# A PEER layer on one NeuronCore: u in hi and lo parts from the first gate group on, one-hot rows made by eight small VectorE operations

## What is computed

```python
q = (t @ q_w).reshape(n, PEER_H, 2, PEER_DQ // 2)
s = einsum('thpd,hpnd->thpn', q, sub_keys)
...                                   # top 16 of the 128 keys on each side, top 16 of their sums
gates = softmax(top_s)
act = gelu(einsum('chkd,cd->chk', u_tab[i_c], x_c))
out = einsum('chk,chkd->cd', g_c * act, v_tab[i_c])
```

## Time and profile before

| | |
|---|---|
| median of 3 runs | 2286.87 us (2285.64 to 2291.26) |
| span of the profiled execution | 2288.8 us |
| busy in it | TensorE 92%, its weight loads 80%, VectorE 60%, ScalarE 42%, GpSimd 10% |
| u loop, first picks to last block | about 1396 to 1910 us |
| of it with gate groups | about 1592 to 1872 us |
| v loop | about 1910 to 2270 us |

### The profile page before, as it was taken

How to read it: one execution, slowest core, us unless ns; L and a number is a source line. 1 busy time by engine, 2 the same in 40 slices (tenths; PEclk the granted TensorE clock), 3 DMA queues, 4 the chain that set the end, 5 groups by cost and what they waited for, 6 DMA issues and landing times.

```text
span 2288.8 us, 34365 instructions
## 1 busy us (share of the span) xinstructions
PE 2108.4 (92%) x12479; PEld 1839.2 (80%) x12479; DVE 1375.4 (60%) x2074; ACT 959.0 (42%) x1885; POOL 234.4 (10%) x219
## 2 busy tenths in 40 slices
PE   6999899977899999879999879999999999999996
PEld 6876788877798879868888778777999988777775
DVE  5535677677766662154544555998555566666665
ACT  4443433458543443133333332112554454555554
POOL 2101000001000000200000000000345551000000
PEclk9999999998999999969999989999999999999998
DMA  7542566644547853300000453444434345666664
GB/s 251 184 183 91 198 236 222 221 148 148 202 159 259 278 184 106 92 29 1 1 1 8 123 109 98 135 137 148 127 122 120 120 120 185 192 187 190 191 187 135
DMA packets 212839, 333.49 MB, mean 146 GB/s; under 512 B 23654, under 2 KB 141148, under 8 KB 212584
## 3 DMA queue, kind: packets, MB, share of 16 engines
q1 hardware_dynamic: 209320, 321.20, 44.2%
q0 software_dynamic: 3392, 10.52, 1.3%
HBM read 330.58 MB, written 1.08 MB: 145 GB/s over the span
## 4 chain that ended last, share of the span: by engine, by line
PE 68%; DVE 16%; PEld 7%; ACT 3%; issue 3%; DMA 1%; SPq 1%; PEldq 1%; DVEq 0%; ACTq 0%
PE psum L2204 14%; PE psum L2205 14%; PE psum L2206 14%; PE psum L2725 10%; PEld psum L2204 2%; PEld psum L2205 2%; PE psum L2766 2%; PEld psum L2206 2%; DVE weights_lo L1546 2%; PE psum L2616 2%; PE psum L2622 2%; DVE u_turned L2145 1%; DVE u_turned_more L2145 1%; PE psum L2597 1%; DVE top_at L2079 1%
## 5 line engine op out<-in xcount | busy, mean ns | idle before, releaser
L1546 DVE TENSOR_TENSOR weights_lo<-weights,weights_hi 128x1024 fp32r<-128x1024 f32 (+2 forms) x336 | 345.3, 1085 | 261.9 <-ACT weights_hi L1078 257.0
L2204 PE MATMUL psum<-input_hi,weights_hi 128*128 128x256 f32 x1288 | 371.6, 289 | 19.1 <-DVE weights_lo L1546 6.1
L2205 PE MATMUL psum<-input_lo,weights_hi 128*128 128x256 f32 x1288 | 367.8, 286 | 0.0
L2206 PE MATMUL psum<-input_hi,weights_lo 128*128 128x256 f32 x1288 | 367.5, 285 | 0.0
L1078 ACT ACTIVATE weights_hi<-weights 128x1024 fp32r<-128x1024 f32 (+2 forms) x336 | 289.2, 931 | 178.3 <-PEq L2251 117.3
L2204 PEld LDWEIGHTS psum<-input_hi,weights_hi 128*128 128x128 f32 x1288 | 250.7, 195 | 34.6 <-issue 32.8
L2205 PEld LDWEIGHTS psum<-input_lo,weights_hi 128*128 128x128 f32 x1288 | 250.9, 195 | 0.0
L2206 PEld LDWEIGHTS psum<-input_hi,weights_lo 128*128 128x128 f32 x1288 | 250.6, 195 | 0.0
L2725 PE MATMUL psum<-input_t,u_turned 128*128 128x256 f32 x912 | 208.3, 383 | 5.5 <-DVE u_turned L2145 3.3
L2725 PE MATMUL psum<-input_t,u_turned_more 128*128 128x256 f32 x896 | 203.2, 381 | 5.3 <-DVE u_turned_more L2145 3.8
L2204 PE MATMUL psum<-v_hi,act_hi 128*128 128x512 f32 x512 | 203.7, 398 | 0.0
(11 more groups left out here) (381 smaller groups left out, 3921.9 us busy)
## 6 DMA issues: line engine op xcount, KB each, us to landing
u_rows<-in_peer_u_dram SPq DMA_DIRECT2D x512, 128.0 KB, 2.5
weights<-in_ffn_w_in_dram SPq DMA_DIRECT2D x44, 1024.0 KB, 7.7
v_rows_even<-in_peer_v_dram SPq DMA_DIRECT2D x64, 512.0 KB, 3.6
v_rows_odd<-in_peer_v_dram SPq DMA_DIRECT2D x64, 512.0 KB, 3.6
weights<-in_ret_w_in_dram SPq DMA_DIRECT2D x24, 1024.0 KB, 7.4
ada_rows_in<-in_ada_w_dram SPq DMA_DIRECT2D x24, 1024.0 KB, 5.3
weights<-in_ffn_w_out_dram SPq DMA_DIRECT2D x44, 512.0 KB, 6.5
weights<-in_lru_w_in_dram SPq DMA_DIRECT2D x12, 1024.0 KB, 6.4
```

The costliest lines, as they stand in the source:

```text
L1546: ins = nc.vector.tensor_tensor(wlo[:, r, at_], wraw[:, r, at_], whi[:, r, at_].bitcast(F32), ALU.subtract)
L2204: nc.tensor.matmul(o, ah, bh, start=start, stop=False)
L2205: nc.tensor.matmul(o, ah, bl, start=False, stop=False)
L2206: return nc.tensor.matmul(o, al, bh, start=False, stop=stop)
```

## The change

Three things are done. `PARTED` goes from 113 to 49, so that the 64 blocks beside which gate groups are made use hi and lo parts too; the blocks from 113 on did so before. ScalarE's `gates_in` and its semaphore `s_ohg` go, and TensorE's gate products wait for VectorE's `s_oh`. The one VectorE operation of 1024 elements becomes eight `tensor_scalar` operations of 128 elements; each takes the place of the pick, and on the first side also the gate, as a scalar column of `HKT`, and those of the first side compare and multiply in one.

```diff
--- before.py
+++ after.py
@@ -353,7 +353,7 @@
 
 GROUPS = S // 4
 GROUP_FIRST = len(PICKS) + 3
-PARTED = GROUP_FIRST + GROUPS
+PARTED = GROUP_FIRST
 
 
 def plain_buffer(j):
@@ -658,7 +658,6 @@
         s_pe = sem("s_pexp")
         s_pk = sem("s_pk")
         s_oh = sem("s_oh")
-        s_ohg = sem("s_ohg")
         s_ht = sem("s_ht")
         s_ur = [sem(f"s_ur{b}") for b in range(2)]
         s_vr = [sem(f"s_vr{b}") for b in range(4)]
@@ -1459,15 +1458,6 @@
                 act.wait_ge(s_ap, max(j - 1, PARTED))
                 nc.scalar.activation(UTH[:, b, :, :], UT[:, b, :, :], ACT.Copy).then_inc(s_uh[b], 1)
 
-            def gates_in(g):
-
-                act.wait_ge(s_oh, g + 1)
-                for x in range(4):
-                    one = ONE[:, g % 2, 0, x, :]
-                    t = 4 * g + x
-                    ins = nc.scalar.activation(one, one, ACT.Copy, scale=HKT[:, 2, t:t + 1])
-                ins.then_inc(s_ohg, 1)
-
             def gelu(j):
 
                 act.wait_ge(s_ap, j + 1)
@@ -1502,8 +1492,6 @@
                         .then_inc(s_hk, 1)
                 if group_made(j - 2) is not None:
                     gates_out(group_made(j - 2), j + 1)
-                if group_made(j) is not None:
-                    gates_in(group_made(j))
 
             def high(j, i=0):
 
@@ -2163,10 +2151,11 @@
                     dve.wait_ge(s_hk, TT)
                 if g >= 2:
                     dve.wait_ge(s_gf, g - 1)
-                both = [P, 2, 4, P]
-                iota = IOTA[:, :].unsqueeze(1).unsqueeze(1).broadcast_to(both)
-                places = HKT[:, 0:2, 4 * g:4 * g + 4].unsqueeze(3).broadcast_to(both)
-                nc.vector.tensor_tensor(ONE[:, g % 2], iota, places, ALU.is_equal).then_inc(s_oh, 1)
+                for x in range(4):
+                    place = lambda q: HKT[:, q, 4 * g + x:4 * g + x + 1]
+                    nc.vector.tensor_scalar(ONE[:, g % 2, 0, x, :], IOTA[:, :], place(0), place(2), ALU.is_equal, ALU.mult)
+                    ins = nc.vector.tensor_scalar(ONE[:, g % 2, 1, x, :], IOTA[:, :], place(1), None, ALU.is_equal)
+                ins.then_inc(s_oh, 1)
 
             def beside(j):
 
@@ -2761,7 +2750,7 @@
 
                 if g >= 2:
                     pe.wait_ge(s_ge, g - 1)
-                pe.wait_ge(s_ohg, g + 1)
+                pe.wait_ge(s_oh, g + 1)
                 for x in range(4):
                     ins = nc.tensor.matmul(PS[:, 6 + g % 2, x * P:(x + 1) * P], ONE[:, g % 2, 1, x, :],
                                            ONE[:, g % 2, 0, x, :], start=True, stop=True)
```

## The result

The changed kernel takes 2332.8 us, median of 4 runs (2323.8 to 2336.4), against 2287.0 beside it: a ratio of 1.019, 95% interval 1.017 to 1.021. The profiled execution has a span of 2331.9 us, 43.1 above the one of before.

What follows compares the result with a forecast made beforehand. TensorE bounds the gate-group stretch at 4.34 us a block; VectorE's 4.23 with 1.1 of stalls makes 5.33. So 2288.8 + 64 x (5.33 - 4.34) = 2352.2, forecast 2350 us, range 2282 to 2386.

Steps and rivals of the forecast that it cites:

- the changeover paid once: The plain-to-parted changeover, with TensorE's two waits of 1 to 2 us, moves from block 113 to 49, paid as before.
- VectorE's own work: Blocks 49 to 112: one-hots 1.95, transposition 1.17 and lo part 1.11 make 4.23 us a block, above TensorE's.
- The price of the one-column form: VectorE's small one-hot operation with one scalar column: about 0.23 us, from a row of four at 0.295 each.
- The stalls: VectorE and GpSimd keep each other out in blocks 49 to 112, adding 1.1 us a block to VectorE's 4.23.
- That the small operations take the lock: The eight one-hot operations take the port pair VectorE shares with GpSimd, by the skill's rule for two-port modes.
- The first rival: Small operations leave the lock alone, or GpSimd slips into the transpositions: period 4.6, 2304 us (2281 to 2326); chance 0.20.
- The price of 0.13 us: The skill's figure for one small VectorE one-hot operation, 1.0 us for the eight; the forecast took 1.95 instead.
- the fourth rival: Cheap small operations, GpSimd's work falling into VectorE's idle time and transposition; TensorE bound at 3.9: 2259 us; chance 0.08.
- the third: Small operations cost about 0.14 us, VectorE 3.4 plus stalls 4.35 a block: no change, 2287 us (2265 to 2310); chance 0.12.
- TensorE's 3.9: TensorE's work per block in 49 to 112: 24 fp32r passes 2.9 plus one-hot products 1.0, 0.44 less than 4.34.
- ScalarE, costed at nothing: ScalarE loses gate multiplications (1.26 us), gains a hi copy (1.05), keeps well over 1 us free a block: no cost.

Runs made afterwards that it cites:

- the first part alone: Kernel before with only PARTED moved to 49 (hi and lo parts), one 1024-element one-hot operation and ScalarE's gate multiplications kept: 2326.0 us, ratio 1.017.

## Why the prediction was right, and where it was off

**The direction and the place.** It said that VectorE becomes the bound and that GpSimd's multiplications are added to its work. VectorE's 310.00 of 310.00 us show the first, the pair with GpSimd's work cut the second: 4.08 us a block without it, 5.00 with it. The time, 2333, lies in the range; the forecast of 2350 is 17 too high, from two terms that were both too large. With the measured period the forecast's own sum gives 2288.8 + 64 x (5.00 - 4.34) = 2331, against the 2331.9 measured, so its other terms (the changeover paid once, nothing for ScalarE, the clock or the loads) hold: the granted clock stayed at 1.00 and the DMA share fell from 0.40 to 0.34.

**VectorE's own work:** forecast 4.23, measured 4.07. The transposition (1.17, measured 1.16) and the lo part (1.11, 1.10) were right. The eight operations were put at 1.95 and take 1.81: 0.195 with one column (forecast 0.23) and 0.26 with two (0.26). The price of the one-column form came from the mean of a merged row, and that row has a hitch in it: its four operations start at 1067.84, 1068.11, 1068.46 and 1068.73, and of the 16 such distances of this line in the whole trace 15 are 0.26 to 0.27 and only this one is 0.36. With 0.265 in place of 0.295 the same working gives 0.20, which is the price measured. 64 x 0.16 = 10 us of the miss.

**The stalls:** forecast 1.10 us a block, measured 0.93, 64 x 0.17 = 11 us. The periods by place were 4.95, 5.37 and 5.66 in the forecast and 4.61, 5.09 and 5.59 in the trace. The forecast's start was too dear (0.72 of stalls, measured 0.54) and its end slightly too cheap (1.43, measured 1.52). The pattern at the end was wrong: not 4.23 and 7.09 in turn but 5.6 each time, with the lo part held for 0.45 (1.63 against 1.18) and the first small operation for 1.05 (1.39 against 0.34). That the mean at the end still came within 0.1 us is luck in part: the forecast placed both multiplications behind the lo part in one block and both ahead of it in the next, and the trace has one on each side in every block. Why it settles so was not tried.

**That the small operations take the lock,** which rested on the Trainium skill (SBUF — State Buffer, section "SBUF: two separate sides") and on no row: the trace agrees. They are stretched from 0.28 to 1.35 us in the changed kernel and to 1.43 in plain blocks without lo parts, and with GpSimd's work cut none takes over 0.48. The first rival, which let them off, falls. That they run in a two-port mode no run here shows by itself.

**The price of 0.13 us** by the Trainium skill (VectorE: DVE Perf Modes, section "The TRN2 errata") is what the operation costs with constants, 0.133 start to start. The page has no price for the columns, which add 0.06 and 0.13. At that price the change would have been faster: the run with constants is 1.1% under before, at 2266 us between the fourth rival's 2259 and the third's 2287, with the fourth's state in its first 51 periods and stalls in the last 12. So these rivals had a price that does not hold with columns, but the right condition, VectorE's work with its stalls against TensorE's.

**TensorE's 3.9** is 3.76: 2.86 for the 24 passes (forecast 2.9) and 0.90 for the gate products (forecast 1.0, their distance to the plain pass behind them). It doesn't enter the result.

**ScalarE, costed at nothing:** right for the change as a whole, where its order has only the hi copy left. But the reason given, that ScalarE has over 1 us free, would have misled for the first part alone: there ScalarE had free time too (busy 165.19 of 250 us), and yet the chain through it took 4.66 us a block.

## What to carry to other kernels

An engine's idle time is not all there to be spent when it and another engine keep each other out: count in the other's instructions as far as they fall beside operations that have to wait for them, since the same instructions in another order gave back some 38 of 43 us. Ahead of replacing one wide operation by several narrow ones, price them from rows with the same kind of operands, and from the distances of single starts, not from the mean of a merged row; here one scalar column made these half as dear again and two twice as dear, and the set costs 0.66 us more than the operation it replaced. And look for the chain from an engine back to itself through the others: taking a step off it (here the gate multiplications, moved by one place in ScalarE's order) gained some 68 us over the first part alone, where taking GpSimd's work away had gained 15.

## What was not expected of the hardware

A scalar column costs VectorE time even where operations follow one another without a wait: starts 0.133 us apart with constants, 0.195 with one column, 0.26 with two, for 128 elements of float32. And the turns are not always one instruction each. In the run of the changed kernel with GpSimd's work cut, the 64 group multiplications are of a single element each, and 29 of them take under 0.5 us but 31 over 0.8. One of the long ones reads:

```profile
1704.16 1.33 POOL L1050 TENSOR_TENSOR act_table<-act_table,gates 128x1 f32<-128x1 f32 x1 [0.48 <-ACT act_table L1480]
```

It ends at 1705.49, when VectorE's eight small operations are through (1705.43), while in the block of the changed kernel shown above GpSimd gets in after the first of them. What decides whether it gets in between two small operations was not tried.
